# Where the adaLN modulation rows are multiplied: TensorE in the layer openings, or VectorE inside the branch merges

## The chip, the cores and the metric

The program runs on one core of one Trainium2 chip. The metric is device time in microseconds (us). TensorE does matmuls, VectorE (DVE), ScalarE (ACT) and GpSimd (POOL) do element-wise work, and SyncE (SP) issues most transfers.

## The reference

Two layers run over 768 tokens (512 latent, 256 context) of width 1024. In each layer `silu(c) @ w_ada[l] + b_ada[l]` gives a row of 3072 values, once for the latents and once for the context:

```
mod_lat = (silu(c) @ w_ada[l] + b_ada[l])
mod_ctx = silu(c_ctx) @ w_ada[l] + b_ada[l]
u_c, gate_c = adaln_modulate(h_ctx, mod_ctx)     # layer_norm(h) * (1 + scale) + shift, gate
u_x, gate_x = adaln_modulate(h_lat, mod_lat)
... four branches (gdn, hyena, gqa, diff) from u @ w_in, merged by sigmoid gates, times w_out
new_lat = post_norm(h_lat, gate_x * out_x, ln_g[l], ln_b[l])
if want_ctx: h_ctx = post_norm(h_ctx, gate_c * out_c, ...)   # first layer only
```

The 3072 columns are six chunks of 512: chunks 0 and 1 are the shift, 2 and 3 the scale, 4 and 5 the gate. Shift and scale are needed before the layer's first projection, the gate only behind its last one. In the second layer the context row of the gate is not needed.

## The kernel before, in words

Every engine runs its own instruction list, in order, and they meet through semaphores. Tokens lie along the free axis in the projections (`u_hi`, `u_lo`), 768 in the first layer and 512 in the second. A weight tile of 128x1024 is loaded into one of three `raw` buffers (`pieces` on SP, L737), then split on ScalarE (`t_whi`, L1775) and GpSimd (`t_wlo`, L973) into one of three slots, and TensorE makes three matmuls of it (L1012 to L1014). SP issues the load of tile n only when the split of tile n-3 is done, and a slot is rewritten only when TensorE has used the tile three before.

`opening(l)` (L84) writes out the order of the work ahead of a layer. "ada" is one 512 KB piece of `w_ada`: a chunk of 512 columns has four such pieces, and each is two matmuls in plain float32 with `cs` (the silu of both conditioning vectors) as the weights (L1152). Behind the fourth, `row` (L2396) adds the bias, "turn" (L1162) transposes shift and scale chunks, and `modulation` (L2402) writes them to `mod`. Between these stand the Hyena filter's spectrum ("tap", "blk", "put"), the layer norms ("sum", "nrm", "gain", "stat", "unit") and "u", which applies `mod` and splits the result. "blk" is L1198 on TensorE for the latents, "tap" is L1136, the transposes of "u" are L1106.

Behind each of the four branches stands `merge(l, n)`. TensorE projects four tiles for the branch's output gate (three in branch 0 of the first layer, one in the second) and one more tile for the merge gate, then waits for all four `mg_y`, and goes through four tiles `p` of `w_br`, each in two halves `dd`, so eight halves k = 2p + dd. Half k writes PSUM banks 4 and 5 (dd = 0) or 6 and 7 (dd = 1) and may only start when VectorE has taken half k-2 out of them (`mg_acc`). VectorE makes `t_yv`, `t_b_hi`, `t_b_lo` for j = 0 to 3, then per half a product with the gate and (from branch 1 on) a sum into `acc`. SP's part is `gate_loads` (L833). In it the load of `w_in` or `w_br` at d = 6 and the two behind it are already the next phase's first three tiles, and behind `gate_loads` SP waits for a fence at the end of the merge.

Of the kernel before, what the change touches and what calls it, by code (L numbers as in the profile page):

```python
# [36 lines left out]
RAW, CONV = 3, 3  # L37
LEVELS = 7
# [45 lines left out]
def opening(l):  # L84

    if l == 0:
# [34 lines left out]
        yield "ada", 4, 0  # L121
        yield "ada", 4, 1
# [4 lines left out]
        yield "ada", 4, 2  # L127
        yield "ada", 4, 3
# [5 lines left out]
        yield "ada", 5, 0  # L134
        yield "ada", 5, 1
# [3 lines left out]
        yield "ada", 5, 2  # L139
        yield "ada", 5, 3  # L140
# [15 lines left out]
    for q in range(4):  # L156
        yield "ada", 0, q
        if q % 2:
            yield "sum", 3 + q // 2, 0
    yield "nrm", 3, 0  # L160
    yield "turn", 0, 0
    for q in range(4):
        yield "ada", 1, q
        if q == 1:
            yield "sum", 5, 0
            yield "nrm", 4, 0
            yield "gain", 3, 0
    yield "nrm", 5, 0
    yield "gain", 4, 0
    yield "stat", 0, 0  # L170
    yield "turn", 1, 0
    for t in range(4):
        yield "tap", 0, t
        yield "ada", 2, t
        if t == 0:
            yield "gain", 5, 0
        else:
            yield "stat", t, 0
    yield "turn", 2, 0
    yield "blk", 0, 0  # L180
    yield "stat", 4, 0
    yield "tap", 1, 0
    yield "ada", 3, 0
    yield "blk", 0, 1
    yield "stat", 5, 0
    yield "tap", 1, 1
    yield "ada", 3, 1
    yield "put", 0, 0
    yield "blk", 0, 2
    yield "tap", 1, 2  # L190
    yield "ada", 3, 2
    yield "put", 0, 1
    yield "tap", 1, 3
    yield "ada", 3, 3
    yield "turn", 3, 0
    for q in range(4):
        yield "ada", 4, q
        if q > 1:
            for i in range(3 * q - 6, 3 * q - 3):
                yield "unit", i, 0  # L200
    yield "blk", 1, 0
    for q in range(4):
        yield "ada", 5, q
        yield "u", q, 0
        if q == 0:
            yield "blk", 1, 1
        if q == 1:
            yield "put", 1, 0
            yield "blk", 1, 2
        if q == 2:  # L210
            yield "put", 1, 1
# [143 lines left out]
def trunk(nc, A, out):  # L355
    es = ExitStack()
    with es:
        def sb(name, shape, dt=f32, stack=es):
# [3 lines left out]
                 "ada_silu", "ada_row", "ada_t", "ada_mod",  # L362
                 "f_mlp", "f_arg", "f_sin", "f_h4", "f_sd", "f_w4", "f_fo", "f_oc", "f_ev", "f_stage",
                 "ln_var", "ln_sd", "ln_n", "ln_x", "ln_t", "ln_u", "ln_split",
                 "cv_tap", "cv_done", "cv_silu", "q_sq", "q_sum", "q_sum_ok", "kv_t", "kv_tok",
                 "k_sum", "k_sd", "k_norm", "k_t", "k_t_ok", "k_t_dve", "ab_w", "ab_ps", "ab_f", "ab_t", "ab_z", "ab_act", "ab_g",
# [70 lines left out]
        cs = sb("cs", [P, KT, 2])  # L437
        oT = sb("oT", [P, BT, TOK])
# [99 lines left out]
        with ExitStack() as m:  # L538
            b_hi, b_lo = sb("b_hi", [P, BT, TOK], f32r, m), sb("b_lo", [P, BT, TOK], f32r, m)
            sil = sb("sil", [P, 2, TOK], stack=m)  # L540
            yv = sb("yv", [P, TOK], stack=m)
            sg = sb("sg", [P, KT, TOK], stack=m)
            sil_s = sb("sil_s", [P, max(SCAN_SILU), TOK], stack=m)
        with ExitStack() as m:
# [141 lines left out]
        SCAN_PHASES = NT * 11  # L686

# [43 lines left out]
        def _(sp):  # L731
# [139 lines left out]
            for l in range(DEPTH):  # L871
# [4 lines left out]
                pieces(3)  # L876
                fenced(f0 + 2)
# [106 lines left out]
        def _(pe):  # L984
# [250 lines left out]
            def gdn_project(l, gates):  # L1235
# [15 lines left out]
                for j in range(12):  # L1251
# [210 lines left out]

            def merge(l, n):
# [5 lines left out]
                project(full, "mg_sg")  # L1469
                ln.take("mg_y", BT)  # L1470
                for p in range(4):
                    hi, lo = piece()
                    for dd in range(2):
# [8 lines left out]
                        lend("mg_acc", 2 * i, 2 * i + 1)  # L1482

# [281 lines left out]
        def _(act):  # L1765
# [102 lines left out]
            def open_layer(l):  # L1868
# [6 lines left out]
                for kind, a, b in opening(l):  # L1875
# [36 lines left out]
                    if kind == "put":  # L1912
# [6 lines left out]
                        splits_due()  # L1919
# [17 lines left out]
                    if kind == "u":  # L1937
                        if a == 0:
# [11 lines left out]
            def gdn_project(l, evacs):  # L1950
# [8 lines left out]
                for j in range(12):  # L1959
# [13 lines left out]
                    if j == 2:  # L1973
                        act.wait_ge(sems["ab_z"], l + 1)
# [371 lines left out]
        def _(dve):  # L2346
# [49 lines left out]
            def row(l, n):  # L2396

                dve.wait_ge(bada_ld[n % 2], 16 * (3 * l + n // 2 + 1))
                dst = mrow[:, n % 2, :] if n < 4 else grow[:, (n - 4) * 512:(n - 3) * 512]
                ln.done(tt(dst, ps[0:2, 6 + n % 2, :], bada[:, n % 2, :], ALU.add), "ada_row")  # L2400
# [66 lines left out]
            def open_layer(l):  # L2467
                g = groups(l)
                dve.wait_ge(sems["ld_par"], 256 if l else 96)
# [96 lines left out]
            def gdn_project(l):  # L2566
# [18 lines left out]
                def log_decay_argument():  # L2585
# [7 lines left out]
                    ln.done(tt(g[2], g[0], g[1], ALU.max), "ab_z")  # L2593
# [238 lines left out]
            def merge(l, first, last=False):  # L2832
# [445 lines left out]
```

## Time and profile before

| | us |
|---|---|
| median of 3 runs | 2761.46 (2755.3 to 2765.77) |
| span of the profiled execution (first to last instruction) | 2761.2 |
| TensorE matmul busy in it | 2632.7 (95%) |
| VectorE busy | 1542.8 (56%) |
| ScalarE busy | 947.1 (34%) |
| GpSimd busy | 560.8 (20%) |

The profiled execution has no other time than its span. In the profile a line such as "x4" groups instructions that follow each other, a number in brackets is the time in which the engine stood idle before them, with what ended it. A float32 matmul shows as two records. Matmuls overlap, so a run of them is timed from one start to the next.

### The profile page before, as it was taken

What the parts mean: (1) busy time and instruction counts of PE and PEld (TensorE: products, weight loads), DVE (VectorE), ACT (ScalarE), POOL (GpSimd) and SP (SyncE); (2) the same over time, 40 slices, a digit from 0 to 9 for tenths busy, and PEclk for the clock granted to TensorE, in tenths of its full rate; (3) what the DMA queues carried; (4) which work ended last, traced back from release to release, by engine and by line L of the source; (5) the groups of instructions that cost most, each with busy time, mean ns of one, the idle gap of its engine ahead of it and who ended that gap; (6) DMA issues with size and microseconds to landing.
All of it is one profiled execution on the core that took longest, in us unless ns stands there. A gap on an engine that the chain in (4) does not pass through costs nothing.

```text
span 2761.2 us, 50245 instructions
## 1 busy us (share of the span) xinstructions
PE 2632.7 (95%) x21342; PEld 2268.3 (82%) x21342; DVE 1542.8 (56%) x2752; ACT 947.1 (34%) x1498; POOL 560.8 (20%) x232
## 2 busy tenths in 40 slices
PE   7899999999999999999999989899999999999998
PEld 1399888899999999997897538888778788888776
DVE  5755777427654443434647764668738643352656
ACT  0335333322322343224532233443343334433541
POOL 0122000120113211321023502200131132242032
PEclk9999999999999999999999999999999999999999
DMA  7421000332222112220134552100153331332033
GB/s 251 160 75 48 16 30 24 110 117 97 81 89 90 61 54 102 79 91 33 34 120 150 192 197 78 47 26 26 42 181 109 113 106 53 109 115 69 24 122 115
DMA packets 95165, 250.97 MB, mean 91 GB/s; under 512 B 11010, under 2 KB 32516, under 8 KB 94432
## 3 DMA queue, kind: packets, MB, share of 16 engines
q1 hardware_dynamic: 84170, 219.56, 23.9%
q10 hardware_dynamic: 10774, 28.19, 2.9%
q8 instruction: 171, 2.80, 0.4%
q14 instruction: 50, 0.41, 0.0%
HBM read 205.12 MB, written 35.26 MB: 87 GB/s over the span
## 4 chain that ended last, share of the span: by engine, by line
PE 84%; DVE 8%; ACT 3%; issue 2%; DMA 2%; SPq 0%; ACTq 0%; DVEq 0%
PE ps L1012 19%; PE ps L1014 19%; PE ps L1013 19%; PE ps L1020 6%; PE ps L1029 3%; PE ps L1041 2%; PE ps L1638 2%; PE ps L1152 2%; PE ps L1669 2%; PE ps L1652 2%; PE ps L1666 2%; PE ps L1198 1%; DVE t_gcv L2366 1%; PE ps L1106 1%; DMA t_raw<-in_w_ada 1%
## 5 line engine op out<-in xcount | busy, mean ns | idle before, releaser
L973 POOL TENSOR_TENSOR t_wlo<-t_raw,t_whi 128x1024 fp32r<-128x1024 f32 x217 | 534.1, 2462 | 2125.9 <-ACT t_whi L1775 2125.8
L1012 PE MATMUL ps<-t_u_hi,t_whi 128*128 128x384 f32 (+1 forms) x2368 | 845.5, 357 | 17.6 <-ACT t_oT L1846 6.7
L1014 PE MATMUL ps<-t_u_hi,t_wlo 128*128 128x384 f32 (+1 forms) x2368 | 825.9, 349 | 0.0
L1013 PE MATMUL ps<-t_u_lo,t_whi 128*128 128x384 f32 (+1 forms) x2368 | 825.1, 348 | 0.0
L1775 ACT ACTIVATE t_whi<-t_raw 128x1024 fp32r<-128x1024 f32 x235 | 248.3, 1057 | 773.9 <-PE ps L1014 704.7
L1012 PEld LDWEIGHTS ps<-t_u_hi,t_whi 128*128 128x128 f32 x2368 | 445.8, 188 | 52.7 <-issue 19.5
L1014 PEld LDWEIGHTS ps<-t_u_hi,t_wlo 128*128 128x128 f32 x2368 | 445.3, 188 | 23.7
L1013 PEld LDWEIGHTS ps<-t_u_lo,t_whi 128*128 128x128 f32 x2368 | 446.3, 188 | 21.0 <-issue 0.5
L1846 ACT ACTIVATE t_grp<-ps 128x256 f32<-128x256 f32 (+2 forms) x192 | 80.6, 435 | 232.5 <-PE ps L1029 134.5
L1012 PE MATMUL ps<-t_b_hi,t_whi 128*128 128x384 f32 (+1 forms) x384 | 137.7, 358 | 6.3 <-DVE t_acc L2358 3.4
L2366 DVE SCALAR_TENSOR_TENSOR t_gcv<-ps,t_par,t_gcv 128x128 f32<-128x128 f32 (+8 forms) x192 | 84.8, 494 | 98.0 <-ACT t_gcv L1846 96.2
L1014 PE MATMUL ps<-t_b_hi,t_wlo 128*128 128x384 f32 (+1 forms) x384 | 136.7, 356 | 0.0
L1013 PE MATMUL ps<-t_b_lo,t_whi 128*128 128x384 f32 (+1 forms) x384 | 136.3, 355 | 0.0
L2358 DVE TENSOR_TENSOR t_yv<-t_oT,t_sil 128x768 f32<-128x768 f32 (+1 forms) x28 | 58.6, 2092 | 133.1 <-ACT t_sil L1846 133.0
L3048 DVE TENSOR_REDUCE t_amx<-ps 128x1 f32<-128x768 f32 (+1 forms) x80 | 64.3, 843 | 98.6 <-PE ps L1638 98.1
L2366 DVE SCALAR_TENSOR_TENSOR t_hcv<-ps,t_par,t_hcv 128x384 f32<-128x384 f32 (+3 forms) x96 | 48.3, 546 | 115.2 <-ACT t_hcv L1846 114.2
L1152 PE MATMUL ps<-t_raw,t_cs 128*2 128x512 f32 x192 | 93.5, 624 | 7.6 <-DMA t_raw<-in_w_ada 7.6
L1846 ACT ACTIVATE t_prob<-ps,t_amx 128x768 f32<-128x768 f32 (+1 forms) x80 | 64.6, 812 | 90.4 <-DVE t_amx L3048 88.5
L2700 DVE COPY_PREDICATED t_grp<-t_masks,ps 128x256 f32<-128x256 uint8 x120 | 53.3, 444 | 66.7 <-PE ps L1029 61.1
L2358 DVE TENSOR_TENSOR t_yv<-ps,t_sg 128x768 f32<-128x768 f32 (+1 forms) x48 | 39.5, 824 | 89.9 <-PE ps L1014 89.8
L1012 PEld LDWEIGHTS ps<-t_b_hi,t_whi 128*128 128x128 f32 x384 | 72.6, 189 | 13.7 <-DVE t_acc L2358 4.5
L1846 ACT ACTIVATE t_pT<-ps 128x768 f32<-128x768 f32 (+2 forms) x108 | 78.9, 731 | 2.0 <-PE ps L1652 1.9
(322 smaller groups left out, 3926.7 us busy)
## 6 DMA issues: line engine op xcount, KB each, us to landing
t_raw<-in_w_in SPq DMA_DIRECT2D x184, 512.0 KB, 3.6
t_raw<-in_w_ada SPq DMA_DIRECT2D x48, 512.0 KB, 4.5
t_raw<-in_w_br SPq DMA_DIRECT2D x32, 512.0 KB, 3.8
t_raw<-in_w_out SPq DMA_DIRECT2D x24, 512.0 KB, 3.8
t_sg<-gate_logits SPq DMA_DIRECT2D x28, 384.0 KB, 4.3
hs<-t_hstage ACTq DMA_DIRECT2D x20, 512.0 KB, 4.5
t_hring<-hs SPq DMA_DIRECT2D x20, 512.0 KB, 6.1
t_prob<-t_pT ACTq DMA_DIRECT2D x56, 128.0 KB, 2.1
```

What stands on the lines that cost most here:

```text
L973: pool.tensor_tensor(lo, raw[:, s % RAW, :], hi.bitcast(f32), ALU.subtract)\
L1012: pe.matmul(o, lh, rh, start=first, stop=False)
L1013: pe.matmul(o, lh, rl, start=False, stop=False)
L1014: return pe.matmul(o, ll, rh, start=False, stop=last)
L1020: last = pe.matmul(ps[:, bank, c], lhs(h, c), rhs(h, c), start=True, stop=True)
L1029: last = pe.matmul(ps[r, bank, c], lhs[r, a], rhs[r, c], start=True, stop=True)
L1152: last = pe.matmul(ps[0:2, 6 + a % 2, :], cs[:, k, :], r[:, kk * 512:(kk + 1) * 512], start=k == 0, stop=k == KT - 1)
L1775: act.activation(conv_slot(c)[0], raw[:, s % RAW, :], ACT.Copy).then_inc(sems["w_hi"], 1)
L1846: return act.activation(o, i, f, **kw)
L2358: return dve.tensor_tensor(o, a, b, op)
L2366: return dve.scalar_tensor_tensor(out=o, in0=a, scalar=s, in1=b, op0=op0, op1=op1)
L3048: ln.done(dve.reduce_max(bias, slot(i % 2)[:, 0:nk], AX.X, negate=True), "at_max")
```

## The change

The second layer's six chunks and the first layer's chunks 4 and 5 leave the openings (32 of 48 pieces of `w_ada`). They go into the merges by a table: in merge (0,0) chunk 0 of layer 1 and chunk 4 of layer 0, in (0,1) chunk 1 and chunk 5 of layer 0, in (0,2) and (0,3) chunks 2 and 3, in (1,1) and (1,2) the second layer's gate chunks 4 and 5. A piece is loaded into the one buffer `mraw`, VectorE multiplies its rows by the conditioning value of the partition and adds them up in `msum`, and when four pieces are in, TensorE sums over the partitions with small float32 matmuls. VectorE then adds the bias, which for the second layer's shift and scale lies transposed in `bcol`. The second layer's opening gets a new order without "ada" and "turn".

```diff
+SUMMED_IN = {(0, 0): ((1, 0), (0, 4)), (0, 1): ((1, 1), (0, 5)), (0, 2): ((1, 2),), (0, 3): ((1, 3),),
+             (1, 1): ((1, 4),), (1, 2): ((1, 5),)}
+SECOND_AT = (0, 2, 4, 5)
...
     # opening(1)
-    for q in range(4):
-        yield "ada", 0, q
...
+    yield from (("sum", 3, 0), ("tap", 0, 0), ("sum", 4, 0), ("nrm", 3, 0), ("tap", 0, 1), ("sum", 5, 0))
+    yield from (("nrm", 4, 0), ("gain", 3, 0), ("tap", 0, 2), ("nrm", 5, 0), ("gain", 4, 0), ("stat", 0, 0))
+    yield from (("tap", 0, 3), ("gain", 5, 0), ("stat", 1, 0), ("tap", 1, 0), ("stat", 2, 0), ("tap", 1, 1))
+    yield from (("stat", 3, 0), ("stat", 4, 0), ("blk", 0, 0), ("tap", 1, 2), ("stat", 5, 0), ("blk", 0, 1))
+    yield from (("tap", 1, 3), ("unit", 0, 0), ("put", 0, 0), ("unit", 1, 0), ("blk", 0, 2), ("unit", 2, 0))
+    yield from (("unit", 3, 0), ("put", 0, 1), ("unit", 4, 0), ("unit", 5, 0), ("blk", 1, 0), ("u", 0, 0))
+    yield from (("blk", 1, 1), ("u", 1, 0), ("put", 1, 0), ("blk", 1, 2), ("u", 2, 0), ("u", 3, 0), ("put", 1, 1))
...
     # SP
+            def modulation_piece(coming):
+                for L, a, b in coming:
+                    q = chunks_loaded[0]
+                    chunks_loaded[0] += 1
+                    if q:
+                        sp.wait_ge(sems["md_used"], q)
+                    x = A["w_ada"][L, a, b].rearrange("p (k c) -> p k c", k=2)
+                    sp.dma_start(mraw[:, :, :], x).then_inc(bada_ld[0], 16)
+                    return
             def gate_loads(l, n):
+                coming = iter([(L, a, b) for L, a in SUMMED_IN.get((l, n), ()) for b in range(4)])
+                if l == 0 and n == 0:
+                    x = A["b_ada"][1][0:1, 0:2 * D].rearrange("a (j p) -> p (a j)", p=P)
+                    sp.dma_start(bcol[:, :], x, allow_slow_non_contiguous=True).then_inc(bada_ld[1], 16)
...
+                modulation_piece(coming)
                 stored_by(stored[0])
...
                     pieces(1 if d >= x else 0)
+                    if 4 <= d < 7:
+                        modulation_piece(coming)
                 pieces(1)
+                for _ in range(4):
+                    modulation_piece(coming)
...
     # TensorE
+            def across_partitions(L, a, bank):
+                summed_chunks[0] += 1
+                pe.wait_ge(sems["ada_row"], GATE_CHUNK + summed_chunks[0])
+                claim(bank)
+                rows = summed_rows(L, a)        # (0,) for the second layer's gate, else (0, 1)
+                if a < GATE_CHUNK:
+                    for j in range(4):
+                        for v in rows:
+                            last = pe.matmul(ps[:, bank, 2 * j + v:2 * j + v + 1], msum[:, v, j * P:(j + 1) * P],
+                                             ones[:, 0:1], start=True, stop=True)
+                else:
+                    for v in rows:
+                        last = pe.matmul(ps[0:2, bank, :], pick[:, v:v + 2], msum[:, v, :],
+                                         start=v == 0, stop=v == rows[-1])
...
                 project(full, "mg_sg")
+                chunks = SUMMED_IN.get((l, n), ())
+                for L, a in chunks[:1]:
+                    across_partitions(L, a, 7)
                 ln.take("mg_y", BT)
...
+                        if (p, dd) == (3, 0):
+                            for L, a in chunks[1:]:
+                                across_partitions(L, a, 0)
...
     # VectorE
+            def add_piece(L, a, b):
+                dve.wait_ge(bada_ld[0], 16 * (macs[0] + 1 + GATE_CHUNK // 2))
+                macs[0] += 1
+                for k in range(2):
+                    for v in summed_rows(L, a):
+                        x, y, c = mraw[:, k, :], msum[:, v, :], cs[:, 2 * b + k, v:v + 1]
+                        if b == 0 and k == 0:
+                            ins = ts(y, x, c, None, ALU.mult)
+                        else:
+                            ins = stt(y, x, c, y, ALU.mult, ALU.add)
+                    ln.step(ins, "md_used" if k else "dve_step")
+                if b == 3:
+                    ln.done(dve.drain(), "ada_row")
...
                     ln.step(tt(b_lo[:, j, 0:w], yv[:, 0:w], b_hi[:, j, 0:w].bitcast(f32), ALU.subtract), "mg_y")
+                    for L, a in chunks[:1]:
+                        add_piece(L, a, j)
...
+                for L, a in chunks[:1]:
+                    summed_out(L, a, 7)
...
                             # at the end of the work of half k
+                        for L, a in chunks[1:]:
+                            if k in SECOND_AT:
+                                add_piece(L, a, SECOND_AT.index(k))
+                            if k == 6:
+                                summed_out(L, a, 0)
```

## Rows read from the trace of the kernel before

**Rows 1.** The page: busy time by engine; the group of the modulation matmuls.

```profile
PE 2632.7 (95%) x21342; PEld 2268.3 (82%) x21342; DVE 1542.8 (56%) x2752; ACT 947.1 (34%) x1498; POOL 560.8 (20%) x232
...
L1152 PE MATMUL ps<-t_raw,t_cs 128*2 128x512 f32 x192 | 93.5, 624 | 7.6 <-DMA t_raw<-in_w_ada 7.6
```

**Rows 2.** TensorE in order of time, second opening (start us, us).

```profile
1615.14 7.22 PE L1152 MATMUL ps<-t_raw,t_cs 128*2 128x512 f32 x16
```

**Rows 3.** Window: start:end, us, busy us (instructions) by engine, PEclk, DMA share, GB/s.

```profile
1561.20:1657.15 95.95, 83.12 (x240) 28.00 (x239) 67.08 (x103) 28.37 (x41) 12.35 (x6) 0.97 0.61 214
```

**Rows 4.** Groups of 1559 to 1657: busy us, mean ns, idle before, releaser.

```profile
L2366 DVE SCALAR_TENSOR_TENSOR t_hstage<-ps,t_sd_ctx 128x1024 f32<-128x1024 f32 x8 | 9.4, 1219 | 4.5 <-PE ps L1198 4.5
L1846 ACT ACTIVATE t_acc<-t_acc,t_nmr,t_rstd 128x1024 f32<-128x1024 f32 x6 | 7.0, 1230 | 13.9 <-DVE t_nmr L2363 13.9
...
L2358 DVE TENSOR_TENSOR t_mrow<-ps,t_bada 2x512 f32<-2x512 f32 x4 | 2.7, 676 | 4.1 <-PE ps L1152 4.1
```

**Rows 5.** ScalarE and VectorE in order of time, end of the first opening.

```profile
110.79 1.06 ACT L1775 ACTIVATE t_whi<-t_raw 128x1024 fp32r<-128x1024 f32 x1 [9.55 <-DMA t_raw<-in_w_in]
...
117.56 2.36 DVE L2366 SCALAR_TENSOR_TENSOR t_sd_ctx<-ps,t_sd_ctx 128x1024 f32<-128x1024 f32 x2 [5.08 <-ACT t_sd_ctx L1846]
```

**Rows 6.** SP in order of time: merges (0,0), (0,1) and (1,1).

```profile
552.51 39.54 SPq L745 DMA_DIRECT2D t_raw<-in_w_in  x4
...
843.07 17.72 SPq L745 DMA_DIRECT2D t_raw<-in_w_in  x3
...
2204.71 0.33 SPq L745 DMA_DIRECT2D t_raw<-in_w_br  x1
...
2210.15 11.69 SPq L745 DMA_DIRECT2D t_raw<-in_w_in  x3
```

**Rows 7.** VectorE in order of time: merges (0,0), (0,1) and (1,1).

```profile
561.54 0.96 DVE L2358 TENSOR_TENSOR t_acc<-ps,t_sg 128x768 f32<-128x768 f32 x1 [6.65 <-PE ps L1014]
...
841.38 2.48 DVE L2358 TENSOR_TENSOR t_yv<-t_oT,t_sil 128x768 f32<-128x768 f32 x1 [4.26 <-ACT t_sil L1846]
...
852.09 0.96 DVE L2358 TENSOR_TENSOR t_yv<-ps,t_sg 128x768 f32<-128x768 f32 x1 [6.64 <-PE ps L1014]
...
856.22 0.96 DVE L2358 TENSOR_TENSOR t_yv<-ps,t_sg 128x768 f32<-128x768 f32 x1 [2.18 <-PE ps L1014]
...
2215.08 0.69 DVE L2358 TENSOR_TENSOR t_yv<-ps,t_sg 128x512 f32<-128x512 f32 x1 [3.22 <-PE ps L1014]
```

**Rows 8.** GpSimd in order of time: merges (0,0) and (0,1).

```profile
566.74 2.41 POOL L973 TENSOR_TENSOR t_wlo<-t_raw,t_whi 128x1024 fp32r<-128x1024 f32 x1 [5.91 <-ACT t_whi L1775]
...
840.65 2.39 POOL L973 TENSOR_TENSOR t_wlo<-t_raw,t_whi 128x1024 fp32r<-128x1024 f32 x1 [5.93 <-ACT t_whi L1775]
848.97 2.41 POOL L973 TENSOR_TENSOR t_wlo<-t_raw,t_whi 128x1024 fp32r<-128x1024 f32 x1 [5.93 <-ACT t_whi L1775]
857.29 3.14 POOL L973 TENSOR_TENSOR t_wlo<-t_raw,t_whi 128x1024 fp32r<-128x1024 f32 x1 [5.91 <-ACT t_whi L1775]
```

**Rows 9.** DMA issues of the page: count, KB each, median us to landing.

```profile
t_raw<-in_w_ada SPq DMA_DIRECT2D x48, 512.0 KB, 4.5
t_raw<-in_w_br SPq DMA_DIRECT2D x32, 512.0 KB, 3.8
```

**Rows 10.** VectorE in order of time, 128x512 float32 in SBUF.

```profile
1521.52 2.14 DVE L2366 SCALAR_TENSOR_TENSOR t_net<-t_net 128x512 f32<-128x512 f32 x3
1523.70 0.43 DVE L2363 TENSOR_SCALAR t_net<-t_net 128x512 f32<-128x512 f32 x1
```

**Rows 11.** TensorE in order of time, float32 matmuls of one column.

```profile
2289.62 0.95 PE L1604 MATMUL ps<-t_cst,t_prob 128*128 128x1 f32 x8
2290.43 0.42 PE L1012 MATMUL ps<-t_u_hi,t_whi 128*128 128x384 f32 x1
```

**Rows 12.** Windows, columns as in rows 3: around an idle stretch of TensorE.

```profile
116.00:120.00 4.00, 0.38 (x4) 0.14 (x2) 2.41 (x3) 3.77 (x6) 3.79 (x2) 0.93 0.00 0
120.00:124.00 4.00, 3.94 (x5) 1.85 (x6) 2.89 (x4) 0.00 (x0) 0.00 (x0) 0.50 0.00 0
```

More of the change, by code:

```diff
@@ L437, in trunk @@
         cs = sb("cs", [P, KT, 2])
+        bcol = sb("bcol", [P, 16])
+        pick = sb("pick", [P, 4])
         oT = sb("oT", [P, BT, TOK])
@@ L543, in trunk @@
             sil_s = sb("sil_s", [P, max(SCAN_SILU), TOK], stack=m)
+            mraw = sb("mraw", [P, 2, 512], stack=m)
+            msum = sb("msum", [P, 2, 512], stack=m)
         with ExitStack() as m:
@@ L686, in trunk, with summed_rows @@
         SCAN_PHASES = NT * 11
+        def summed_rows(L, a):
+            return (0, 1) if a < GATE_CHUNK or L == 0 else (0,)
         def gate_units(l):
@@ L2396, in row @@
             def row(l, n):
-                dve.wait_ge(bada_ld[n % 2], 16 * (3 * l + n // 2 + 1))
-                dst = mrow[:, n % 2, :] if n < 4 else grow[:, (n - 4) * 512:(n - 3) * 512]
-                ln.done(tt(dst, ps[0:2, 6 + n % 2, :], bada[:, n % 2, :], ALU.add), "ada_row")
+                dve.wait_ge(bada_ld[n % 2], 16 * (n // 2 + 1))
+                ln.done(tt(mrow[:, n % 2, :], ps[0:2, 6 + n % 2, :], bada[:, n % 2, :], ALU.add), "ada_row")
             def modulation(n):
@@ L2592, in log_decay_argument @@
                     step(ts(g[3], g[0], 0.0, None, ALU.max))
-                    ln.done(tt(g[2], g[0], g[1], ALU.max), "ab_z")
+                    ln.done(tt(g[2], g[0], g[1], ALU.max), "ab_g")
                 def log_decay():
@@ L2830, in out_norm, with summed_out, merge @@
                     ln.done(tt(x, x, r, ALU.mult), "on_x")
-            def merge(l, first, last=False):
+            macs, rows_out = [0], [0]
+            def add_piece(L, a, b):
[11 more added lines that the diff above has]
+                    ln.done(dve.drain(), "ada_row")
+            def summed_out(L, a, bank):
+                ln.take("ada_t")
+                if a >= GATE_CHUNK:
+                    rows_out[0] += 1
+                    dve.wait_ge(bada_ld[1], 16 * (rows_out[0] + 1 + GATE_CHUNK // 2))
+                    c = slice((a - GATE_CHUNK) * 512, (a - GATE_CHUNK + 1) * 512)
+                    ln.done(tt(grow[:, c], ps[0:2, bank, :], grow[:, c], ALU.add), "ada_mod")
+                    return
+                if a == 0:
+                    dve.wait_ge(bada_ld[1], 16 * (2 + GATE_CHUNK // 2))
+                t = ps[:, bank, 0:8].rearrange("p (j r) -> p j r", r=2)
+                b = bcol[:, 4 * a:4 * a + 4].unsqueeze(2).broadcast_to([P, 4, 2])
+                if a < 2:
+                    ln.done(tt(mod[:, 4 * a:4 * a + 4, :], t, b, ALU.add), "ada_mod")
+                else:
+                    ln.done(stt(mod[:, 4 * a:4 * a + 4, :], t, 1.0, b, ALU.add, ALU.add), "ada_mod")
+            def merge(l, n):
+                first, last = n == 0, n == 3
+                chunks = SUMMED_IN.get((l, n), ())
                 w = width(l == 0)
@@ L3146, in _ @@
                 fence(ln, "dve")
-                merge(l, True)
+                merge(l, 0)
                 fence(ln, "dve")
@@ L3150, in _ @@
                 fence(ln, "dve")
-                merge(l, False)
+                merge(l, 1)
                 fence(ln, "dve")
@@ L3154, in _ @@
                 fence(ln, "dve")
-                merge(l, False)
+                merge(l, 2)
                 fence(ln, "dve")
@@ L3159, in _ @@
                 fence(ln, "dve")
-                merge(l, False, True)
+                merge(l, 3)
                 fence(ln, "dve")
```

100 lines of the change are left out of this document (26 added, 74 removed).

## The prediction

> **What bounds the kernel now.** I read the page first: TensorE is busy for 95% of the span and nothing else comes near [rows 1]. So the question for every edit is whether TensorE issues less, and whether it waits for something new. The group of L1152 on the same page is what the change is about. For its price I then took TensorE in order of time, where pieces stand back to back: 16 records, which are four pieces, take 7.22 us, so 1.8 us a piece [rows 2]. The reader should see that the clock is full there and no operand is waited for. Then I went through both openings and the merges engine by engine, SP's list and the landing times included, because the moved pieces get one buffer and a chain of their own.
>
> **What is removed.** 32 pieces x 1.8 = 57.6 us of TensorE. Whether that comes back depends on what else fills the openings.
>
> *Second opening.* It lasts 95.95 us from VectorE's first to its last work, and VectorE is busy in 67.08 of them [rows 3]. Of these some 4.6 are bias adds (six of 0.68 [rows 4]) and small copies that leave. So VectorE's own floor is 62.5 us and the most that can be won is 33.5. The new order does not reach it. I walked it through item by item, each operation with the duration it has in the old opening (a blk, for one, costs VectorE two of 1.22 [rows 4]). VectorE has no gap until stat 4, 31 us in. From blk 0 on it alternates: TensorE's product, ScalarE's copy, VectorE, then TensorE again, and the six `unit` activations of ScalarE (1.23 each [rows 4]) stand ahead of the second group's blk. That walk ends 14.5 us before the old end, an estimate. The bounds are 8, if TensorE, now idle half the time, runs all its products there at the low clock, and 33.5.
>
> *First opening.* Eight pieces, 14.4 us, and ScalarE's wait of 9.55 for the first `w_in` tile [rows 5] go. Filter products, `unit` and the three splits remain ahead of the copy that blk 3 waits for, at 117.56 now [rows 5]. By the same walk that becomes some 110, less what the low clock takes: 5.5, with bounds 2 and 14.4.
>
> Together 20.0 us are won, by TensorE's removed work up to 57.6.
>
> **What is added in the merges, first chunk.** Nothing of this is in the trace of before, so I time it from its neighbours. A piece costs VectorE four operations of 128x512. Three such take 2.14 us and the single-input form 0.43 [rows 10], so I take 2.7 us for two rows and 1.4 for one. That is hidden for j = 0 to 2, since VectorE idles 4.26 us before each product [rows 7]. The last piece is not. SP issues it at d = 6 behind the next phase's tile, 843.07 in merge (0,1) [rows 6], so at 843.4. Landing takes 4.5, the median of the same source [rows 9]; the bounds are 3.8, a weight tile of that size alone [rows 9], and 5.3, an estimate of as much above 4.5 as 3.8 is below it, since two loads of 512 KB then share the engines. It lands at 847.9 and is added by 850.6. TensorE ends its gate projection at 852.09 less one half. A half lasts 856.22 - 852.09 = 4.13 [rows 7], which gives 847.9. `across_partitions` stands there, ahead of all of `w_br`, and waits for the row: 2.7 us. In merge (0,0) the same sum is 552.51 + 0.4 + 4.5 + 2.7 = 560.1 against 561.54 - 4.13 = 557.4 [rows 6, 7], again 2.7.
>
> It will be somewhat more. GpSimd starts a split at 848.97 [rows 8], within these adds. Where VectorE's product met a split (841.38 for 2.48 us, the split 840.65 for 2.39) it ended with it, though the same shape takes 0.96 elsewhere; and where VectorE was first, the split took 3.14 instead of 2.41 [rows 7, 8]. So the third add can be held for up to 2.4 us, and I take 1.3 of it: 4.0 a merge. The Trainium skill (SBUF — State Buffer, on the port pair that VectorE and GpSimd share) says that an operation with two SBUF inputs and a GpSimd read exclude each other for the whole instruction; the trace agrees, and by it alone each wait would be 5.1 and the whole forecast 4.4 us higher.
>
> Then come the small matmuls. Eight records of one column take 0.81 us [rows 11], so the 16 of a shift or scale chunk 1.6. And the clock: TensorE, busy for 0.38 us from 116 to 120, was granted 0.50 in the 4 us behind it [rows 12]. That is the 1.2 GHz level and costs 2 us of work. The pauses here are of about that length or a little shorter, so I take 1.2, between 0 and 2. Four merges x (4.0 + 1.6 + 1.2) = 27.2.
>
> *Second layer, (1,1) and (1,2).* Here a projection lasts only 5.4 us. SP comes to the last piece at 2210.6, but VectorE frees the buffer only at 2211.0, since piece 2 goes out behind 2204.71 and lands at 2209.6 [rows 6, 9]. So the last one lands at 2215.5 and is added by 2216.9. TensorE is done at 2212.35, one half (4.13 x 512/768 = 2.75) ahead of 2215.08 [rows 7]. That is 4.6, with a split in the way 5.6. Two x (5.6 + 0.9 for two records of 512 columns + 1.2) = 15.4.
>
> **Second chunk, (0,0) and (0,1).** This is the largest term. Its four loads stand behind all tiles of `gate_loads`. The third of the next phase's tiles goes out with the end of GpSimd's split at 857.29 + 3.14 = 860.43 [rows 8], in agreement with 843.07 + 17.72 [rows 6]. Half 1 ended at 856.2, call that T. So piece 0 is issued at T + 4.6, lands at T + 9.1 and is added by T + 11.8. But VectorE has stood in that wait since half 0, in front of its work on half 1, which needs two operations of 0.96 [rows 7], another 1.95 with the gap. TensorE's half 3 writes the banks of half 1, so it starts at T + 13.8 rather than T + 4.15: a stall of 9.7. In (0,0) the split ends at 569.15 [rows 8], T + 3.6, and only one operation follows: 8.0. From there each piece needs a round trip (release, 4.5 to land, 2.7 to add). Carried on half by half, the last piece is in 3.6 and 4.0 us after TensorE has reached the second `across_partitions`. With 1.8 for four records of 512 columns: 15.1 + 13.8 = 28.9, and 2.3 in each for the low clock: 33.5.
>
> **The rest.** `bcol` is 2048 single values. No row shows such a load. It is free if it hides (nothing in (0,0) but the first piece hangs on it), and up to 8 if it holds that piece back by two landings: 2. The Trainium skill (DMA: Bandwidth & Descriptors) says that a non-contiguous last dimension makes one descriptor per element; no run so far shows it. The bias rows of 4 KB and VectorE's final adds are small and beside TensorE. The renamed `ab_g` changes nothing. SP's blocked queue costs nothing behind the last tile, as a fence follows anyway.
>
> Sum: 27.2 + 15.4 + 33.5 + 2 = 78.1 lost, 20.0 won. 2761.2 + 58.1 = 2819.3 of span. The span stands 0.3 under the median of the runs, so I give 2819.6.
>
> **Rivals.** (1) The second chunk hides: were its pieces in the buffer when VectorE comes to them, the 33.5 would shrink to 3.6 of matmuls: 2789. For it: VectorE idles 2.18 before each half [rows 7]. Against: SP's order. (2) TensorE gets all of its 57.6 back: 2819.3 - 37.6 = 2782. For it: TensorE's 95%. Against: VectorE's floor [rows 3] and ScalarE's chain. (3) Other side, faster: the adds are in before TensorE asks, so that the merges cost only 11.8 us of matmuls (6.4 + 1.8 + 3.6). With openings at 40 won (33.5 + 6.5) it is 2733, with my 20 it is 2753. It decides at 4.5 - 2.7 = 1.8 us from issue to landing for the last piece; the shortest median here is 3.8 [rows 9]. (4) Worse: two loads share the engines (5.3 to land, ten waits, +8), the lock holds every late add (+4.4), `bcol` +6, openings only 10 (+10): 2848.
>
> **How the numbers follow.** Forecast 0.58, (1) 0.15, (2) 0.05, (4) 0.10, (3) at 2753 0.06 and at 2733 0.06. A measurement of this kernel tells 0.5% (13.8 us) from no change. Slower is then 0.88, the same 0.06, faster 0.06. The range for 8 in 10 goes from (2) to (4): 2780 to 2848. The likeliest case alone would be 2800 to 2840.
>
> **What would show it.** L1152 falls from 192 to 64 records. The second opening, from the last `w_out` product to the first projection, shrinks from 96 to about 81. In the six merges of the table TensorE is idle before the float32 matmuls on `msum`, released by VectorE or by the load into `mraw`. In (0,0) and (0,1) there is a gap of 8 to 10 us before half 3 and one of some 4 behind half 6. Landing of `mraw` is 4 to 5 us. The prediction fails if these gaps are missing (then the loads go out earlier than I read from SP's list), or if the openings shrink by far more than 20.

## The result

| | us |
|---|---|
| forecast | 2819.6 (2780 to 2848) |
| after, median of 4 runs | 2850.13 (2847.36 to 2856.25) |
| before, beside it | 2758.38 |
| ratio, with its 95% interval | 1.0331 (1.0313 to 1.035) |
| span of the profiled execution of after | 2849.5 |

Slower, as forecast, but by 91.8 us instead of 58.1: 2 us outside the range.

The page of after, to be read beside [rows 1, 9]: the span, busy time by engine, the chain that ended last, the group of VectorE's adds, and the issues of the moved pieces (count, size).

```profile
span 2849.5 us, 50255 instructions
PE 2629.9 (92%) x21274; PEld 2292.3 (80%) x21274; DVE 1627.4 (57%) x2862; ACT 946.7 (33%) x1498; POOL 562.0 (20%) x232
...
PE 75%; DVE 13%; DMA 5%; ACT 3%; issue 3%; SPq 0%; POOL 0%; ACTq 0%; DVEq 0%
...
L2375 DVE SCALAR_TENSOR_TENSOR t_msum<-t_mraw,t_cs,t_msum 128x512 f32<-128x512 f32 x98 | 90.9, 963 | 39.1 <-DMA t_mraw<-in_w_ada 37.7
...
t_mraw<-in_w_ada SPq DMA_DIRECT2D x32, 512.0 KB
```

TensorE's busy time fell by 2.8 us, though 57.6 us of pieces left: the sums brought 24 us of records, and records at half clock last double. What matters is the chain. In before it was TensorE for 84%; now it is 75%, and VectorE has 13% in place of 8%.

TensorE's waits in after, largest first (engine, tile and line, releaser: us in all, times, longest):

```profile
PE ps L1456 <- DVEq L2858: 25.1, 4, 6.3
PE ps L994 <- DVE t_acc L2367: 18.5, 4, 8.9
PE ps L1460 <- DVEq L2858: 18.3, 4, 6.7
```

L1456 and L1460 are the sums over the partitions, L2858 is VectorE's end of a chunk, and the second line is mostly the two halves behind a late second chunk, one in (0,0) and one in (0,1) (its other two waits are 1.4 and 0.4; before has three such, 3.4 together):

```profile
578.21 0.66 PE L994 MATMUL ps<-t_b_hi,t_whi 128*128 128x384 f32 x1 [7.76 <-DVE t_acc L2367]
...
898.90 0.66 PE L994 MATMUL ps<-t_b_hi,t_whi 128*128 128x384 f32 x1 [8.93 <-DVE t_acc L2367]
```

To see where time goes, I took VectorE's record at the same points of both traces and subtracted. This is worked out from its rows in order of time; "half 0" and "half 7" are the starts of its first and last product with the gate in a merge, and "gdn" is its last masked copy in that branch, ahead of merge (0,0). Columns: lag behind before, in us (minus is ahead).

```
point                         after    e1    e2    e3    e4    e6    e9
end of the first opening       -6.2  -5.0  -7.0   0.0  -4.9  -8.2  +1.1
late in gdn, layer 0           -5.6  -4.3  -4.5  +3.0  -4.5  -5.6  +0.4
first b_lo of (0,0)           -10.8  -9.5  -8.1  -1.1  -8.1 -10.9  -4.2
half 0 of (0,0)                +0.7  -9.4  -6.0  +9.9  +4.2  -6.3  -4.5
half 7 of (0,0)               +17.0  -8.8 +11.5  +9.9 +18.0  +1.5  -2.6
half 0 of (0,1)               +29.7  -8.6 +13.7 +22.1 +30.7 +14.0  -2.5
half 7 of (0,1)               +48.2  -8.1 +36.1 +22.2 +49.3 +24.6  -0.6
half 7 of (0,2)               +61.0  -7.2 +42.3 +33.8 +62.1 +29.9  +1.7
half 7 of (0,3)               +73.3  -6.0 +50.2 +44.7 +74.4 +32.9  +2.3
end of the second opening     +65.0 -12.0 +43.1 +36.4 +59.7 +25.0  -9.1
half 7 of (1,0)               +67.8  -9.0 +46.4 +38.6 +62.6 +28.8  -6.7
half 7 of (1,1)               +81.1  -6.9 +58.8 +52.5 +77.5 +41.8  -2.8
half 7 of (1,2)               +91.4  -6.4 +65.0 +62.8 +88.2 +50.8  -0.7
last work of VectorE          +88.7 -11.5 +59.7 +58.3 +82.8 +45.6  -4.4
```

Up to merge (0,0) after won 10.8 and in the second opening 8.3, together 19.1. But only 6.2 of the 10.8 are there at the end of the first opening. Another 5.3 appear between the second and the third row, where the two kernels do the same, and they come from a stall in the one profile of before. TensorE stands 1.92 us for nothing that the profile shows ("issue"), and 6 us at half clock follow. TensorE in order of time, and the window behind it:

```profile
487.36 0.27 PE L1041 MATMUL ps<-t_grp 64*64 64x64 f32 x1 [1.92 <-issue]
...
489.00:495.00 6.00, 6.00 (x36) 5.54 (x36) 2.67 (x9) 0.38 (x1) 0.00 (x0) 0.51 0.01 3
```

After has no such wait there and keeps full clock. So every column of the table stands some 3 to 5 us too well from the third row on, and the openings' own win in after is 6.2 + 8.3 = 14.5. The second chunks, half 0 to half 7 of (0,0) and (0,1), cost 16.3 + 18.5 = 34.8. The six first chunks cost 11.4, 12.7, 12.8, 12.3, 13.3 and 10.3, together 72.8, where the forecast had 42.6.

One of them, (0,2), in order of time: VectorE, then SP, GpSimd and TensorE.

```profile
1159.12 0.96 DVE L2367 TENSOR_TENSOR t_b_lo<-t_yv,t_b_hi 128x768 fp32r<-128x768 f32 x1
1163.63 3.34 DVE L2375 SCALAR_TENSOR_TENSOR t_msum<-t_mraw,t_cs,t_msum 128x512 f32<-128x512 f32 x4 [3.56 <-DMA t_mraw<-in_w_ada]
1167.00 0.96 DVE L2367 TENSOR_TENSOR t_yv<-t_oT,t_sil 128x768 f32<-128x768 f32 x1
1167.99 0.56 DVE L2890 CAST t_b_hi<-t_yv 128x768 fp32r<-128x768 f32 x1
1168.59 0.96 DVE L2367 TENSOR_TENSOR t_b_lo<-t_yv,t_b_hi 128x768 fp32r<-128x768 f32 x1
1170.45 4.80 DVE L2375 SCALAR_TENSOR_TENSOR t_msum<-t_mraw,t_cs,t_msum 128x512 f32<-128x512 f32 x4 [0.90 <-DMA t_mraw<-in_w_ada]
...
1164.34 0.33 SPq L701 DMA_DIRECT2D t_raw<-in_w_in  x1
1167.00 0.33 SPq L799 DMA_DIRECT2D t_mraw<-in_w_ada  x1
...
1170.24 2.34 POOL L955 TENSOR_TENSOR t_wlo<-t_raw,t_whi 128x1024 fp32r<-128x1024 f32 x1 [5.93 <-ACT t_whi L1783]
...
1175.35 3.58 PE L1456 MATMUL ps<-t_cst,t_msum 128*128 128x1 f32 x16 [6.27 <-DVEq L2858]
```

Read it backwards. The sum starts 6.27 us after TensorE went idle, when the last four adds end. They took 4.80, since GpSimd's split (2.34) began 0.2 before them. They began late because the last piece was issued at 1167.00: SP was at it from 1164.7, but the one buffer was free only when the adds before ended, and those had waited 3.56 for their own piece, which took 6.1 from its issue. The landing of the last piece was quick, 3.5. The same loop stands in all six merges: the last two pieces of each first chunk were issued within 0.03 us of the end of the adds before. And in all four merges of the first layer the last adds met a split (4.68 to 4.80).

The clock there (start:end, us, PE, PEld, DVE, ACT, POOL busy, PEclk, DMA share, GB/s):

```profile
1172.00:1176.00 4.00, 0.65 (x3) 0.66 (x4) 3.21 (x4) 0.00 (x0) 0.58 (x1) 0.73 0.39 131
1176.00:1180.00 4.00, 4.00 (x18) 4.00 (x19) 0.17 (x1) 0.00 (x0) 0.00 (x0) 0.50 0.00 0
1180.00:1184.00 4.00, 4.00 (x14) 4.00 (x13) 0.00 (x0) 0.00 (x0) 0.00 (x0) 0.50 0.00 0
1184.00:1190.00 6.00, 6.00 (x36) 6.00 (x36) 2.00 (x3) 0.15 (x1) 0.00 (x0) 0.99 0.01 3
```

8 us at 1.2 GHz is 4 us of work lost: some 1.7 in the sum, which took 3.58, the rest in the first half.

### The profile page after: what moved, and what is told of

Read it like the earlier page. It is cut to its first block, busy times and chain, and to the rows that moved or that the text cites. A ratio compares the mean times of both kernels' runs of the same rounds, so it can differ in the third digit from the quotient of the medians.

```text
span 2849.5 us, 50255 instructions
## 1 busy us (share of the span) xinstructions
PE 2629.9 (92%) x21274; PEld 2292.3 (80%) x21274; DVE 1627.4 (57%) x2862; ACT 946.7 (33%) x1498; POOL 562.0 (20%) x232
## 3 DMA queue, kind: packets, MB, share of 16 engines
q1 hardware_dynamic: 86218, 219.55, 22.9%
## 4 chain that ended last, share of the span: by engine, by line
PE 75%; DVE 13%; DMA 5%; ACT 3%; issue 3%; SPq 0%; POOL 0%; ACTq 0%; DVEq 0%
PE ps L994 17%; PE ps L996 16%; PE ps L995 16%; PE ps L1002 6%; DMA t_mraw<-in_w_ada 3%; DVE t_msum L2375 3%; PE ps L1011 2%; PE ps L1023 2%; PE ps L1646 2%; PE ps L1677 2%; PE ps L1660 2%; PE ps L1674 2%; DVE t_gcv L2375 1%; PE ps L1088 1%; PE ps L1180 1%
## 5 line engine op out<-in xcount | busy, mean ns | idle before, releaser
L994 PE MATMUL ps<-t_b_hi,t_whi 128*128 128x384 f32 (+1 forms) x384 | 146.3, 381 | 21.4 <-DVE t_acc L2367 18.5
L995 PE MATMUL ps<-t_b_lo,t_whi 128*128 128x384 f32 (+1 forms) x384 | 143.6, 374 | 0.0
L996 PE MATMUL ps<-t_b_hi,t_wlo 128*128 128x384 f32 (+1 forms) x384 | 143.2, 373 | 0.0
L2375 DVE SCALAR_TENSOR_TENSOR t_msum<-t_mraw,t_cs,t_msum 128x512 f32<-128x512 f32 x98 | 90.9, 963 | 39.1 <-DMA t_mraw<-in_w_ada 37.7
L2367 DVE TENSOR_TENSOR t_yv<-t_oT,t_sil 128x768 f32<-128x768 f32 (+1 forms) x28 | 35.9, 1282 | 90.2 <-ACT t_sil L1854 89.7
L995 PEld LDWEIGHTS ps<-t_b_lo,t_whi 128*128 128x128 f32 x384 | 78.1, 204 | 5.9
```

Source lines behind the costliest of these rows:

```text
L994: pe.matmul(o, lh, rh, start=first, stop=False)
L995: pe.matmul(o, lh, rl, start=False, stop=False)
L996: return pe.matmul(o, ll, rh, start=False, stop=last)
L2367: return dve.tensor_tensor(o, a, b, op)
L2375: return dve.scalar_tensor_tensor(out=o, in0=a, scalar=s, in1=b, op0=op0, op1=op1)
```

## The experiments

All start from after unless said otherwise. "Ratio" is to before on the same chip.

**e1: openings only.**

```diff
-SUMMED_IN = {(0, 0): ((1, 0), (0, 4)), ...}
+SUMMED_IN = {}
...
+                if l == 0 and first:
+                    step(dve.memset(mod[:, :, :], 1.0))
+                    step(dve.memset(grow[:, :], 1.0))
```

> Openings as changed, no chunk anywhere: the loads, adds and sums in the merges are left out, and the second layer's modulation and all gate rows are set to 1. Both accounts of the loss put it in the merges. By the trace of after the openings and what follows them up to the first merge won 10.8 and 8.6 us, so this should stand about 19 us under before, at 2739. By the rival in which TensorE gets back all that the removed pieces took (57.6) it would be 2701. If taking them out is worth nothing by itself, 2758.

Measured 2751.39, ratio 0.9966 (0.9953 to 0.998). Up to merge (0,0) it stands 9.5 ahead, of which 5.0 are there at the end of the first opening; the second opening wins only 6.0, and the stages between give some back (the table). So with all adds and sums gone, taking 32 pieces from the openings buys 8 us by the medians. The profile has 11.5, with before's stall in it. The rival that TensorE gets back its 57.6 is out.

**e2: the first chunk's sum later.** Behind the first half instead of ahead of it, in bank 1.

```diff
-                for L, a in chunks[:1]:
-                    across_partitions(L, a, 7)
                 ln.take("mg_y", BT)
...
+                        if (p, dd) == (0, 0):
+                            for L, a in chunks[:1]:
+                                across_partitions(L, a, 1)
```

> Only the place of the first chunk's sum is changed: TensorE does it, and VectorE takes it out, behind the first half of the branch products, in bank 1. Theory A: in each of the six merges TensorE stood 5.8 to 6.7 us for the last add, did the sum at half clock (3.6 instead of about 1.6 us) and went on at half clock (some 3): 10 to 11 us each, so 60 to 65 us come back, 2785 to 2790. Rival B: the first chunk costs because VectorE's adds make it late for the halves' own multiplies and for the last branch product; the wait then only moves behind the first half, and less than 20 us come back, 2830 or more.

Measured 2824.86, ratio 1.023 (1.021 to 1.025): 25 back, between the two. The table says why. To half 0, theory A holds: merge (0,1) lost 2.2 there instead of 12.7. Behind it time is lost again. TensorE in order of time and windows in merge (0,2), columns as above:

```profile
1157.46 0.44 PE L994 MATMUL ps<-t_b_hi,t_whi 128*128 128x384 f32 x1 [0.53 <-DVE t_b_lo L2368]
...
1163.25 1.95 PE L1456 MATMUL ps<-t_cst,t_msum 128*128 128x1 f32 x16 [1.35 <-DVEq L2859]
...
1161.00:1165.00 4.00, 2.65 (x22) 2.33 (x20) 3.72 (x6) 0.00 (x0) 0.00 (x0) 1.00 0.42 131
1165.00:1169.00 4.00, 4.00 (x16) 4.00 (x16) 0.47 (x2) 0.00 (x0) 0.00 (x0) 0.57 0.01 4
```

One half of 4.1 us is shorter than what the adds still needed (4.76 in that trace), so TensorE waited 1.35. The sum ran at full clock, 1.95 instead of 3.58, but the clock fell right behind it. In (0,0) and (0,1) half 0 to half 7 took 17.5 and 22.4 instead of 16.3 and 18.5. The late sum stands in these figures; the gaps of the second chunk stayed as they were, 7.9 and 8.9.

**e3: the gate chunks back in the first opening.**

```diff
-SUMMED_IN = {(0, 0): ((1, 0), (0, 4)), (0, 1): ((1, 1), (0, 5)), ...
+SUMMED_IN = {(0, 0): ((1, 0),), (0, 1): ((1, 1),), ...
...
         yield "tap", 3, 0
+        yield "ada", 4, 0
+        yield "ada", 4, 1
...
+        yield "ada", 5, 3
```

> The first layer's two gate chunks are again eight pieces in the first opening; the merges behind gdn and hyena of the first layer keep one chunk each. By the balance of the traces the second chunks took 16.3 and 18.5 us, so 34.8 come back, and the opening gives back 7 to 10 of what it won: 2822 to 2826. Rival: those merges were late for the first chunk and its half clock and the second mostly lies beside the products; then at most 10 us come back in all, 2840 or more.

Measured 2825.46, ratio 1.0233 (1.021 to 1.0257): the forecast number. The second chunks' 34.8 are gone (half 0 to half 7 of (0,0) and (0,1): under 0.1 each), and 9.7 is paid in front of merge (0,0): 6.2 in the opening, the rest in the gdn branch, where the code is the same. The profiles of e7 to e9 show how loose that rest is: their first opening is that of e3, and at the first b_lo they stand 3.1 to 6.1 us better. So part of the hit on 2825 is luck. The first chunks cost what they did, 10.9 to 12.2 a merge in the first layer, with no second chunk near. So the first chunk's cost does not hang on the second.

**e4: the second layer's first splits late.**

```diff
                     c, s = high[0], CONV_AT[high[0]]
+                    if STREAM[s][0] > allowed[0]:
+                        return
...
+                        allowed[0] = l          # at the first "put" of opening(l)
```

> ScalarE does not split the second layer's first three weight tiles before its first stage write of the second opening, so GpSimd does not take them right behind its acc adds. If the 6 us that the second opening won less than forecast are the three VectorE operations of one partition that took 2.4 to 2.7 us beside GpSimd instead of 0.4 to 0.7, this is 6 us faster than after: 2844. If that opening is paced by something else, no change (within 1.5 us).

Measured 2844.83, ratio 1.0305 (1.0284 to 1.0327), 5.3 less. The intervals of the two kernels touch, but the profile has the gain in its place: from (0,3) to the end of the second opening e4 wins 14.7, after 8.3. VectorE and GpSimd there, first after, then e4:

```profile
1658.66 2.71 DVE L2367 TENSOR_TENSOR t_early<-t_sd 1x512 f32<-1x512 f32 x1
1661.40 2.72 DVE L2375 SCALAR_TENSOR_TENSOR t_sd<-t_early 1x512 f32<-1x512 f32 x1
1664.15 2.45 DVE L2371 TENSOR_SCALAR t_sd<-t_early 1x512 f32<-1x512 f32 x1
...
1658.48 7.84 POOL L955 TENSOR_TENSOR t_wlo<-t_raw,t_whi 128x1024 fp32r<-128x1024 f32 x3
```

```profile
1660.66 0.68 DVE L2371 TENSOR_TENSOR t_early<-t_sd 1x512 f32<-1x512 f32 x1
1661.37 0.68 DVE L2379 SCALAR_TENSOR_TENSOR t_sd<-t_early 1x512 f32<-1x512 f32 x1
1662.08 0.41 DVE L2375 TENSOR_SCALAR t_sd<-t_early 1x512 f32<-1x512 f32 x1
...
1682.82 7.00 POOL L955 TENSOR_TENSOR t_wlo<-t_raw,t_whi 128x1024 fp32r<-128x1024 f32 x3 [22.29 <-ACT t_whi L1784]
```

Three splits in a row met three operations on one partition, and each operation waited out one split: 6.1 us.

**e5: one pair of columns in the sum.**

```diff
-                    for j in range(4):
+                    for j in range(1):
```

> In the four merges that sum a modulation chunk TensorE does one pair of one-column products instead of eight (the other columns of the second layer's modulation stay what the bank held: that part of the result is left out). The wait for the adds stays. Theory A, that the wait cools TensorE and the sums only run slow behind it: the sums' 3.6 us fall to about 0.5 at half clock, and the halves behind take some of the half clock that the sums took before, so 2 to 3 us each, 8 to 12 in all: 2838 to 2842. Rival: the one-column products are themselves what keeps the clock low, as the run with the later sum suggests (0.57 right behind a sum that ran at full clock); then the half clock behind them goes too, some 6 us each, 24 in all: 2826.

Measured 2842.11, ratio 1.0307 (1.029 to 1.0325), 8 less, at the edge of theory A's range, and the intervals of the two kernels overlap. The profile has the gain in its place: these four first chunks cost 9.5, 9.9, 9.8 and 8.6 instead of 11.4, 12.7, 12.8 and 12.3, together 11.4 less. The rival's 24 is out. TensorE and the windows at the same place:

```profile
1172.59 1.02 PE L1456 MATMUL ps<-t_cst,t_msum 128*128 128x1 f32 x4 [6.27 <-DVEq L2858]
...
1174.00:1178.00 4.00, 4.00 (x14) 4.00 (x13) 0.00 (x0) 0.00 (x0) 0.00 (x0) 0.51 0.00 0
1178.00:1182.00 4.00, 4.00 (x25) 4.00 (x25) 1.92 (x2) 0.00 (x0) 0.00 (x0) 1.00 0.00 0
```

The wait is the same 6.27 and half clock stands behind it, though hardly any one-column work is left. So an idle stretch of this length is enough to bring it.

**e6: two buffers for the pieces.** The second lies in a part of `sil_s` that these merges don't use.

```diff
-                    if q:
-                        sp.wait_ge(sems["md_used"], q)
+                    if q > 1:
+                        sp.wait_ge(sems["md_used"], q - 1)
...
-                    sp.dma_start(mraw[:, :, :], x).then_inc(bada_ld[0], 16)
+                    sp.dma_start(mraws[q % 2][:, :, :], x).then_inc(sems["ld_const"] if q % 2 else bada_ld[0], 16)
...
+                modulation_piece(coming)        # a second one ahead of the merge
```

> The pieces of w_ada land by turns in two buffers, and two are issued ahead of a merge, so an add no longer waits for a landing that began when the add before it ended. VectorE stood 61 us for these landings in after. If they are what paces the second chunks (four waits of 8.9 us of TensorE ahead of a half) and delays the branch products, 15 to 25 us come back there and some 5 in the six waits at the first chunks: 2820 to 2830. Rival: VectorE's adds themselves, four operations at 1 us and held by GpSimd's splits, set the pace; then less than 8 us.

Measured 2808.48, ratio 1.0183 (1.0161 to 1.0205): 42 back, where I expected 20 to 30. (I had also read the four waits of 18.5 us as 8.9 each; they are 7.8, 8.9 and two small ones.) The second chunks fell from 34.8 to 18.4, the first from 72.8 to 47.4. Merges (0,1) and (0,2) of this one run settle what the adds' length does. TensorE, VectorE's last adds and GpSimd of (0,1), then TensorE and VectorE of (0,2), where no split falls into the last adds, and the window behind that sum:

```profile
855.49 3.57 PE L1459 MATMUL ps<-t_cst,t_msum 128*128 128x1 f32 x16 [4.84 <-DVEq L2862]
...
850.51 4.86 DVE L2378 SCALAR_TENSOR_TENSOR t_msum<-t_sil_s,t_cs,t_msum 128x512 f32<-128x512 f32 x4
...
851.82 2.34 POOL L958 TENSOR_TENSOR t_wlo<-t_raw,t_whi 128x1024 fp32r<-128x1024 f32 x1 [5.92 <-ACT t_whi L1786]
...
1146.10 1.95 PE L1459 MATMUL ps<-t_cst,t_msum 128*128 128x1 f32 x16 [0.64 <-DVEq L2862]
...
1143.13 2.86 DVE L2378 SCALAR_TENSOR_TENSOR t_msum<-t_sil_s,t_cs,t_msum 128x512 f32<-128x512 f32 x4
...
1148.00:1152.00 4.00, 4.00 (x16) 4.00 (x16) 0.17 (x1) 0.00 (x0) 0.98 (x1) 0.58 0.36 128
```

Without the split 2.86 us of adds, a wait of 0.64 and a merge that costs 5.3. With it 4.86, 4.84, and 12.5. The one buffer had made this the rule: from the second piece on every add waited for a landing that began when the one before it ended, and they slid behind VectorE's product onto the splits. With one buffer the last adds were held in four of the first layer's four merges, with two buffers in one. That one, (0,1), shows that the buffer isn't the only way there: its last three groups of adds took 5.08, 5.04 and 4.86 though none waited for a landing. What put them onto the splits was not tested.

**e7: together.** e2, e3 and e4, with the sum behind the second half (in (0,3) the first).

> Sum later (behind the second half, in the last merge of a layer behind the first), gates back in the first opening, splits of the second opening late. If the three gains are independent, 25 + 25 + 5 = 55 and five waits of 1.3 us less: about 2790, so still 1.1% slower than before. If the parts share a cause (gates back already frees VectorE for the first chunks' adds), 2800.

Measured 2775.32, ratio 1.0068 (1.0052 to 1.0084): 75 less than after, where the single gains add up to 55. With two halves ahead of the sum TensorE waits for one sum only, 1.4 us in (0,3), and without the wait the clock holds: the first chunk of (0,2) costs 2.9, in e2 6.1. Another 6.1 of the 20 stand ahead of merge (0,0), where e3 has the same code (7.2 ahead of before at the first b_lo, e3 1.1), and are not a gain of this edit.

**e8: together, and two buffers.**

> As the combined kernel, with two buffers for the pieces. Without second chunks only the adds ahead of the branch products can gain: they delayed b_lo of the last product by 1.5 to 2.8 us a merge through the wait for a landing, so 5 to 12 us less than combined: 2778 to 2785. If that delay is the adds' own time and not the landing, the same as combined.

The edits of e7 and e6 in one kernel. Measured 2766.44, ratio 1.0031 (1.002 to 1.0041), 9 less than e7: TensorE waits 5.2 us for `t_b_lo` in place of 11.3, and for no sum. The sum of (0,2), which TensorE reaches without a wait, and the windows around it:

```profile
1128.75 1.84 PE L1467 MATMUL ps<-t_cst,t_msum 128*128 128x1 f32 x16
...
1128.00:1130.00 2.00, 2.00 (x18) 2.00 (x17) 0.96 (x1) 1.05 (x1) 0.00 (x0) 1.00 0.00 0
1130.00:1132.00 2.00, 2.00 (x15) 2.00 (x15) 1.12 (x2) 0.00 (x1) 1.92 (x1) 1.00 0.00 0
1132.00:1134.00 2.00, 2.00 (x13) 2.00 (x12) 0.00 (x0) 0.00 (x0) 1.21 (x1) 1.00 0.00 0
```

A sum alone costs its 1.84 us and no clock; with 0.64 us of idle ahead of it (e6) or 1.35 (e2) the clock fell to 0.58 and 0.57 behind it. The control for the idle alone stands in the same trace. In merge (1,3) TensorE waits 1.44 with full-width matmuls behind:

```profile
2691.39 0.47 PE L1005 MATMUL ps<-t_b_hi,t_whi 128*128 128x512 f32 x1 [1.44 <-DVE t_acc L2382]
...
2691.00:2695.00 4.00, 3.60 (x16) 2.95 (x17) 3.83 (x8) 0.53 (x1) 0.00 (x0) 1.00 0.39 131
```

So it was the short wait and the narrow matmuls together that cost the clock. A wait of 1.92 with full-width matmuls behind (e9, merge (1,1)) kept 1.00 as well, one of 1.96 (e8, merge (1,2)) did not: 0.71 in the 4 us from 2422.

**e9: e8 with the pieces behind the weight tiles**, and **e10: the same in after.**

```diff
-                modulation_piece(coming)
                 stored_by(stored[0])
...
+                    if d == 2:
+                        modulation_piece(coming)
```

> As the combined kernel with two buffers, but a merge's first two pieces are issued behind its first weight tiles and gate logits instead of ahead of them. In the profile of that kernel the first tile of merge (1,1) landed 6.5 us after its issue (3.8 in before), and TensorE waited 4.4 us for the gate's product because of it; merge (1,2) lost 2.3 us the same way. Theory: these two come back, 5 to 7 us: 2760, which is level with before. Rival: those waits come from something else behind the hyena branch (the spectra, the table load on ScalarE); then no change, and the pieces, now later, may delay the first adds.

> The same single move in the kernel after the change: the first piece (and nothing else) is issued behind the first three weight tiles. Theory: 3 to 6 us back in the second layer's merges (4.5 and 2 us between the last evacuation of a merge and the first branch product of the next), nothing in the first layer: 2845. Rival: none of it, 2850.

e9: 2758.55, ratio 1.0004 (0.9992 to 1.0016), 8 less than e8 and level with before. SP and ScalarE at the start of merge (1,1), e8, then e9:

```profile
2182.01 0.42 SPq L711 DMA_DIRECT2D t_raw<-in_w_in  x1
...
2188.55 1.06 ACT L1796 ACTIVATE t_whi<-t_raw 128x1024 fp32r<-128x1024 f32 x1 [11.05 <-DMA t_raw<-in_w_in]
...
PE ps L1005 <- ACT t_sil L1869: 4.4, 1, 4.4
```

```profile
2182.24 0.41 SPq L711 DMA_DIRECT2D t_raw<-in_w_in  x1
...
2185.96 1.06 ACT L1797 ACTIVATE t_whi<-t_raw 128x1024 fp32r<-128x1024 f32 x1 [7.06 <-DMA t_raw<-in_w_in]
...
PE ps L1006 <- ACT t_sil L1870: 0.4, 1, 0.4
```

The tile lands after 3.7 instead of 6.5 us, and TensorE's wait for the gate goes.

e10: 2850.02, ratio 1.0331 (1.0312 to 1.0349), no change. In its profile merge (1,1) starts 4.0 us better against the end of (1,0), as expected, and gives 1.0 of it back up to half 0, where the pieces are late instead. Up to the end of the second opening this profile stood 2.8 us worse than after's, 1.9 of it before any merge, and at the end 2.8 better. In (1,2) nothing came back (10.6 instead of 10.3). So the delay of the tile is shown, worth 3 us in (1,1), but for after as a whole the move is not shown to be worth anything.

## Why the prediction was wrong

**Right.** The side, and the account that most of the loss is waits and low clock and not the small matmuls. *Second chunk*: 33.5 forecast, 34.8 in the trace, and e3 took it away. The gaps before half 3 were forecast as 9.7 in (0,1) and 8.0 in (0,0) and measured as 8.9 and 7.8; those behind half 6 as 3.6 and 4.0, measured 3.3 and 2.2. *First opening*: 5.5 forecast, 6.2 at its end (4.9 to 8.2 over the seven profiles with the same first opening). TensorE's bound did not help (rival 2): e1 shows it.

**The step that failed: the first chunk**, 27.2 + 15.4 = 42.6 forecast, 72.8 measured. Its parts, for a first-layer merge, here (0,2):

- *The wait*, 4.0 forecast, 6.27 measured. I let the last piece be issued when SP came to it and charged 1.3 for GpSimd's split. In fact the buffer was not free: the adds before had waited for their own piece and run into splits, so the issue was 2.3 late. It landed 1.0 sooner than I took, and the last adds met a split (4.80 instead of 2.86). I had written that adds 0 to 2 hide in VectorE's idle time. Their time hides, but their end is what releases the buffer. In e6, with two buffers, the sums' waits in the first layer fell from 25.1 to 7.1, 4.8 of it in the one merge whose last adds were still held. The price of the split was also misread: I wrote that the product that met a split ended with it, but in the rows of 841.38 it ended 0.8 us behind it, so it had first waited and then run. The Trainium skill (SBUF — State Buffer, Who interferes with whom) has the one that comes second blocked until the other's instruction ends; the rows agree, and the wait that I derived from that rule, 5.1, was nearer to the measured 6.27 than my 4.0.
- *The matmuls*, 1.6 forecast at the full clock of [rows 11], 3.58 measured at half clock. The rows in e2 and e8 (1.95 and 1.84) confirm the price at full clock. I had added a pause's cost to the clock but not priced the work that stands right behind the pause at it.
- *The clock behind*, 1.2 forecast, about 2.3 measured (4 us of lost work in the windows, less the 1.7 inside the sum).
- *Second layer*: 7.7 a merge forecast, 13.3 and 10.3 measured. The waits of 6.1 and 6.7 were near the forecast 5.6; the sums took 1.9 each at half clock instead of 0.9. What was missing altogether was the place of the first load: ahead of the merge's first weight tiles it delays them. In after that was 3 us in (1,1) and nothing in (1,2) (e10); with two pieces ahead (e8 against e9) it was more.

**A smaller miss: the second opening.** 14.5 forecast, 8.3 in the trace. The balance up to merge (0,0) hides it, since before's stall adds 5.3 there. e4 wins 14.7 there and e7 to e9 11.4 to 15.2, so the walk through the order was sound; the missing 6 us are GpSimd's splits. Of them the walk took no account, since in before they stood at other places, behind tiles that came later.

**`bcol`**: 2 forecast, nothing seen. The first piece of (0,0) was issued at 515.3, behind it, and was being added at 519.7, and of the first layer's four first chunks that of (0,0) cost least. The page has 2048 packets more on SP's queue than before (86218 against 84170), as many as `bcol` has values.

**The range.** That 2848, the bound from rival (4), came within 2 us is luck. Of its four surcharges one came true, the lock on late adds (+4.4). The last pieces landed in 3.5 to 4.1 us and not in 5.3, `bcol` cost nothing, and the openings won 14.5 and not 10. The late release of the buffer and the sums at half clock, which cost the time, are not in it.

**Where the gain of 57.6 went.** Of the pieces' 57.6 us the openings hand on 8 by e1's medians; that VectorE and ScalarE pace them is the walk's account, which no run tests by itself. With the splits moved and the waits removed (e9) the medians show no win, and the profile's 4.4 is no more than before's stall. No version with the whole result beat before. Open is why the first opening's win comes out between 4.9 and 8.2 with the same code, what the stall in before's gdn branch is (TensorE waits there for nothing that the profile shows; e8 has one of 1.65 at the same place), and why e1 loses 3.5 us between merges (0,0) and (0,3) with nothing added there.

## What to carry to other kernels

Work moved onto an engine with idle time is free only if its last item is, and with one buffer the end of each item is the start of the next load: follow that loop until it meets something, here the splits of another engine, which hold the item up. Put the consumer that can't wait one or two units of its own work later than the data is due, as e7 did. Price matmuls behind a wait of several us at the clock which the wait leaves. And before a gain is booked to a stage, look whether it is there at that stage's end: half of what seemed the first opening's win was a stall of before's profile.

## What the runs showed of the hardware

- A VectorE operation on a single partition (1x512) was held by a GpSimd split as long as one on 128: 2.71 instead of 0.68 us, where four adds of 128x512 took 4.80 instead of 2.86. The form with one input tensor was held too, 2.45 instead of 0.41. Three such operations met three queued splits, and each waited out one; the splits took 7.84 us together instead of 7.00.
- Half clock stood behind idle stretches as short as 0.64 us when one-column matmuls followed (0.58 in the next 4 us), and not behind the same matmuls without a stretch (1.00), nor behind 1.44 us of idle with matmuls of 512 columns behind (1.00).
- With two loads of 512 KB issued just ahead a weight tile landed in 6.5 us, without them in 3.7 (e8, e9).
